# The low parts of the merge weights of the first two branches, taken from GpSimd to VectorE

## The reference

```python
h = x * (1 + scale) + shift
proj = h @ p['w_in'][l]
hy_in, da_q, da_k, da_v, mla_dq, mla_dkv, mla_kr, paths, merge = jnp.split(proj, IN_SPLITS, axis=-1)
...
br = jnp.stack([y_hy, y_da, y_mla], axis=2) * jax.nn.silu(paths.reshape(b, n, N_BRANCH, BR_W))
y_br = jnp.einsum('blni,nid->blnd', br, p['w_branch'][l])
merged = jnp.sum(jax.nn.sigmoid(merge.reshape(b, n, N_BRANCH, D_MODEL)) * y_br, axis=2)
out = merged @ p['w_out'][l]
x = layer_norm(ALPHA * x + gate * out, p['ln_g'][l], p['ln_b'][l])
```

## Time and profile before

| | |
|---|---|
| median of 3 runs | 1846.05 us |
| lowest and highest | 1843.01 and 1846.44 us |
| the profiled execution | 1844.08 us, of which its span is 1842.3 us |
| mean granted TensorE clock | 0.992 |
| PE busy | 1761.0 us, 96% of the span |
| DVE busy | 1142.0 us, 62% |
| ACT busy | 691.7 us, 38% |
| POOL busy | 481.6 us, 26% |

### The profile page before, as it was taken

One profiled execution on the slowest core, in us unless ns is written; L12 is line 12 of the kernel. 1 busy time (PEld: TensorE's weight loads), 2 busy tenths in 40 slices (PEclk: granted clock), 3 DMA queues, 4 the chain that ended last, 5 costly groups with the idle time before them and its releaser, 6 DMA issues.

```text
span 1842.3 us, 28575 instructions
## 1 busy us (share of the span) xinstructions
PE 1761.0 (96%) x11624; PEld 1579.8 (86%) x11624; DVE 1142.0 (62%) x1626; ACT 691.7 (38%) x1186; POOL 481.6 (26%) x234
## 2 busy tenths in 40 slices
PE   5899999999999999999889999999999999999997
PEld 2888799878898888999876969998888898889997
DVE  5599895455354444587878989925544544435755
ACT  3434312444244455322263332224432454542123
POOL 0100033221242212467301000422222411215563
PEclk9999999999999999999999999999999999999999
DMA  9111122111211111353621112212122111114431
GB/s 361 47 58 35 35 92 75 53 52 56 69 35 54 38 54 58 121 200 120 250 92 35 48 45 68 81 49 62 47 67 65 46 53 39 42 58 160 160 109 69
DMA packets 50594, 150.07 MB, mean 81 GB/s; under 512 B 9690, under 2 KB 13914, under 8 KB 49696
## 3 DMA queue, kind: packets, MB, share of 16 engines
q1 hardware_dynamic: 46864, 134.09, 22.2%
q10 hardware_dynamic: 3600, 14.16, 2.2%
HBM read 141.63 MB, written 6.59 MB: 80 GB/s over the span
## 4 chain that ended last, share of the span: by engine, by line
PE 70%; DVE 19%; issue 5%; ACT 2%; POOL 2%; DMA 1%; ACTq 0%; SPq 0%; DVEq 0%; POOLq 0%
PE PS L888 8%; PE PS L889 8%; PE PS L893 8%; PE PS L908 7%; PE PS L914 6%; PE PS L909 6%; PE PS L997 5%; PE PS L986 4%; PE PS L1010 4%; PE PS L1188 2%; PE PS L1028 2%; PE PS L1031 2%; DVE Wl L1689 2%; POOL Wl L2138 1%; DVE work L1662 1%
## 5 line engine op out<-in xcount | busy, mean ns | idle before, releaser
L2138 POOL TENSOR_TENSOR Wl<-W,Wh 128x1024 fp32r<-128x1024 f32 (+3 forms) x176 | 367.5, 2090 | 1201.7 <-ACT Wh L1312 1201.7
L888 PE MATMUL PS<-Hh,Wh 128*128 128x320 f32 x1472 | 439.5, 313 | 16.4 <-ACT Wh L1312 10.1
L889 PE MATMUL PS<-Hl,Wh 128*128 128x320 f32 x1472 | 435.4, 310 | 0.0
L888 PEld LDWEIGHTS PS<-Hh,Wh 128*128 128x128 f32 x1472 | 278.2, 189 | 32.4 <-issue 18.7
L1668 DVE TENSOR_REDUCE st<-PS 128x1 f32<-128x640 f32 (+1 forms) x160 | 114.9, 718 | 287.1 <-PE PS L1010 184.1
L889 PEld LDWEIGHTS PS<-Hl,Wh 128*128 128x128 f32 x1472 | 278.3, 189 | 0.0
L1312 ACT ACTIVATE work<-PS 128x640 f32<-128x640 f32 (+8 forms) x276 | 170.6, 626 | 262.9 <-PE PS L893 87.4
L893 PE MATMUL PS<-Hh,Wl 128*128 128x320 f32 x1472 | 231.0, 309 | 0.7 <-POOL Wl L2138 0.7
L893 PEld LDWEIGHTS PS<-Hh,Wl 128*128 128x128 f32 x1472 | 219.6, 188 | 1.1 <-POOL Wl L2138 0.9
L1312 ACT ACTIVATE Wh<-W 128x1024 fp32r<-128x1024 f32 (+3 forms) x208 | 186.3, 899 | 78.5 <-PE PS L893 26.7
L908 PE MATMUL PS<-Hh,Wh 128*128 128x320 f32 x544 | 168.8, 324 | 1.9 <-ACT Wh L1312 0.8
(11 more groups left out here) (276 smaller groups left out, 3138.9 us busy)
## 6 DMA issues: line engine op xcount, KB each, us to landing
W<-in_w_in SPq DMA_DIRECT2D x132, 512.0 KB, 3.5
W<-in_w_branch SPq DMA_DIRECT2D x48, 256.0 KB, 2.7
work<-in_w_mod_rows ACTq DMA_DIRECT2D x23, 512.0 KB, 3.8
pmod_w<-in_w_mod SPq DMA_DIRECT2D x8, 1024.0 KB, 11.2
W<-in_w_out SPq DMA_DIRECT2D x16, 512.0 KB, 4.4
work<-in_x_sample SPq DMA_DIRECT2D x2, 2048.0 KB
late_modulation_w<-in_w_mod_rows SPq DMA_DIRECT2D x5, 512.0 KB, 6.6
x_mid<-work SPq DMA_DIRECT2D x1, 2560.0 KB, 8.5
```

Of the source, the lines that this page charges most:

```text
L888: pe.matmul(out, Wh[:, b, kk, :], xh[:, kk, t], start=kk == 0, stop=False)
L889: pe.matmul(out, Wh[:, b, kk, :], xl[:, kk, t], start=False, stop=False)
L2138: return pool.tensor_tensor(out, in_, high.bitcast(f32), ALU.subtract)
```

## The change

`low_by_vector` now also gives VectorE the tiles of `mgate` and `mbranch` with index below `2 * KD` = 16, that is of branches 0 and 1. VectorE makes such a low part at the step `mg0` or `mb0` of its tile, where TensorE begins the Wh products; and it makes only the part of the tile that holds weights (`depth`: 8 blocks of 128 for a gate, 4 for a branch).

```diff
 def low_by_vector(l, n):
-    return n in LOWS or n in (0, 1)
+    return n in LOWS or n in (0, 1) or (SPLIT[n][0] in ("mgate", "mbranch") and SPLIT[n][1] < 2 * KD)
...
                 if l or n > 1:
                     dve.wait_ge(*tile_done(l, n - 2))
-                TT(Wl[:, n % 2], W[:, g % NW], Wh[:, n % 2].bitcast(f32), ALU.subtract).then_inc(sems["w_lo"], 1)
+                k = depth(SPLIT[n][0])
+                TT(Wl[:, n % 2, 0:k], W[:, g % NW, 0:k], Wh[:, n % 2, 0:k].bitcast(f32), ALU.subtract).then_inc(sems["w_lo"], 1)
...
                     if (kind, i) in LOW_BETWEEN:
                         low_part(l, LOW_BETWEEN[kind, i])
+                    if kind in ("mg0", "mb0"):
+                        low_part(l, SPLIT_AT["mgate" if kind == "mg0" else "mbranch", i])
                     if kind == "pmod":
```

## The result

The changed kernel takes **1854.82 us** (median of 4 runs, 1853.64 to 1856.2) beside 1845.23 us of the kernel before (4 runs, 1843.01 to 1846.44). The ratio is **1.0051**, with a 95% interval of 1.0038 to 1.0064: it is slower by 9.6 us, more than the 0.2% that can be told from no change. The forecast said slower, 1853.5 us, in a range of 1848.5 to 1857.5.

What follows compares the result with a forecast made beforehand. The prediction took TensorE to bound the kernel. Waits of 3.5 us (units 4, 9, 14), 3.4 (unit 19) and 0.6 (latent attention) sum to 7.5 us, giving a median of 1853.5 us, range 1848.5 to 1857.5.

Steps and rivals of the forecast that it cites:

- TensorE bound, nothing to win by this: Attention stretches: TensorE is busy nearly throughout and waits for none of the 64 moved tiles, so almost nothing to win.
- Units 4, 9, 14: Differential attention: TensorE waits 0.59 us for VectorE's low part behind the division, six times, 3.5 us.
- the three units show the same 0.19: Units 4, 9, 14, both layers: 0.19 to 0.20 us between the division's end and TensorE's first Wl load.
- Unit 19: Differential attention: low part comes behind two divisions, so TensorE waits 1.7 us, twice, 3.4 us.
- the collision: Unit 19: VectorE's small product takes 2.04 us beside GpSimd's low part; expected gone, else the wait is 3.6 us.
- The 128x512 low part: VectorE's low part on that shape, priced at 0.69 us from the same kind of operation; lower bound 0.61.
- The latent attention: Unit 14: mqr's GpSimd low part comes behind VectorE's, so TensorE waits 0.3 us, twice, 0.6; elsewhere nothing.
- The sum: Whole kernel: 3.5 + 3.4 + 0.6 = 7.5 us slower, all carried to the end.
- The clock behind unit 19: After each 1.7 us wait the granted clock may fall, costing 1.3 us more each, up to 1856.1 us.
- Hidden: Rival: TensorE's queue or an existing wait takes up the delays, or low parts come in time; 1846 to 1849, chance 0.13.
- Faster: Rival: VectorE operations stretched by GpSimd become short and TensorE gains; 1843 us, chance 0.03.
- Dearer: Rival: unit 19's collision stays, both clocks fall, or VectorE's waiting holds up maxima and exponentials; 1856 to 1861, chance 0.12.

Runs made afterwards that it cites:

- the longer low parts: Changed kernel with the eight late branch low parts over all eight blocks (128x1024) instead of four: 1859.79 us, 1.0083 to the kernel before.
- the eight alone: Against the kernel before, VectorE takes only the four branch tiles of each layer wanted in units 4, 9, 14 and 19: 1852.87 us, ratio 1.0042.
- the low parts ahead of the division: Changed kernel with the eight late branch low parts made ahead of VectorE's division instead of behind it: 1847.03 us, 1.0007 to the kernel before.
- branch 1 alone: Against the kernel before, VectorE takes only branch 1's low parts (mgate and mbranch 8 to 15), in the latent attention: 1845.5 us, ratio 1.0.
- a repair: Kernel before, with GpSimd making mv's low part ahead of its part of path 6; alone 1845.49 us, ratio 0.9999.

## Why the prediction was right, and where it was off

**TensorE bound, nothing to win by this: right.** All 64 moved, but in time, gave 1.0007 [0.9997 to 1.0017], and 56 of them 1.0004 [0.9995 to 1.0013]. GpSimd's 116 us less are worth nothing, since TensorE waited for none of these tiles.

**Units 4, 9, 14: 0.59 each, 3.5 in all.** Measured 0.56, 0.55, 0.91, 0.56, 0.68 and 0.56: 3.82 us. Four are right to 0.04. The step that failed a little is "the three units show the same 0.19": in unit 14 of layer 0 VectorE's reduction starts 0.95 us behind the start of the weight load of its matmul (431.73 to 432.68) instead of 0.59, and the low part comes 0.3 us later with it. Two traces of the changed kernel and that of the longer low parts have it, that of the eight alone does not. What causes it is open.

**Unit 19: 1.7 each.** Measured 1.66 twice, with the small product at 0.16 us, as said. That GpSimd's tile, now behind VectorE's, takes the collision out of the way could be read off the order of the two. Had the collision stayed, the wait would have been 3.6 us.

**The 128x512 low part: 0.69.** Measured 0.692; the estimate came from a row of another operation on that shape.

**The latent attention: 0.6.** Measured 0.27 at each load, 0.3 from trace to trace. Nothing else in it waits: unit 2 and the gate tiles had the slack that the rows gave.

**The sum: 7.5 us.** The traces give 7.8 us for the change itself. The medians give 9.6 and 9.8 us, with an interval of about 7.0 to 11.8 us, which holds both. That the forecast of 1853.5 us lies only 1.3 us below the 1854.82 measured is partly luck: it was added to a median of three runs, 1846.05 us, which the fourth run brought to 1845.23, and this 0.8 us hides a part of the 2.1 us by which the sum is short.

The clocks of the runs say where the 2 us are. In the 57 runs of the kernel before that stand beside the experiments the mean granted clock is 0.9897 on average, and a run with a clock lower by 0.001 takes 1.5 us more (a straight line through them, correlation -0.77). The nine runs of the changed kernel have 0.9882 on average; 0.0015 less clock is 2.2 us by this line (an estimate), and of 9.2 us between the means 7.0 are left. The eight low parts alone run at 0.9896, as the kernel before does, and their mean is 7.0 us above it, where the list of loads has 6.6 us of waits. The longer low parts have 0.9880 beside 0.9894: 2.2 us of their 14.3, and 12.1 are left, where the loads have 11.4 and unit 14 of the latent attention 0.5. So, by this estimate, the waits explain what stays at equal clock, and the sum lacks a term for the clock, which the prediction had in its range (up to 1856.1) and not in its sum. No run tests why the clock is lower there. Two candidates are in the traces. One is the start at a lower clock, 2.4 to 3.4 us in two of two traces of the changed kernel, but also in the traces of two kernels as fast as the one before (the low parts ahead of the division, and branch 1 alone). The other is drops of the clock of about 1.5 us, which fall at differing places from trace to trace. The runs do not settle which.

**The clock behind unit 19: not lost.** The page of stretches has 1.00 behind both waits of 1.66 us; the 1.3 us each that I kept in the range did not come. Behind the waits of 2.19 us it came once in two. The term was of the right size, about 1.3 to 1.5 us for a fall of the clock, but it had the place wrong.

**The rivals.** *Hidden* is refuted: the waits are in the time, and each 0.54 us more on the eight comes out at the end. *Faster* is refuted in a telling way: VectorE's stretched operations do become short (2.04 to 0.16 us, 18 us over the program), and nobody waited for them. *Dearer* would have needed the collision or the clock in unit 19, and neither came.

## What to carry to other kernels

Before an instruction is moved to an engine that works in order, compare two times of the trace for each place where it lands: the end of what stands ahead of it there plus its own length, and the start of what consumes it. Here 56 of 64 places had room and cost nothing that the medians show (two of them made a GpSimd tile behind them 0.3 us late); eight had 0.2 us of room or less, and made nearly all of the loss. The busy share of an engine (62% against 26%) says nothing about that. When a late operand is brought forward, another can become the late one: at `mv` VectorE's `kv_lo` was ready at 549.23 us, and at 551.87 us once GpSimd's low part had moved beside it. So look at which engine the moved instruction will now run beside. And a gain that is read off one stretch of two traces needs the stretches around it: the half clock that left unit 16 stood behind `mv`.

## What was not expected of the hardware

- Four operations of VectorE end only after the GpSimd instruction beside them: 3.13 us instead of 0.89 and 2.22 instead of 0.16 in the kernel with the early low parts, 4.99 instead of 2.94 for two at `mv`. I knew it from unit 19, but not that it would undo a repair. The starts do not order them cleanly: the operation of 3.13 us begins 0.03 us ahead of GpSimd's, and is stretched all the same.
- The length of a wait alone does not tell whether the clock falls. TensorE's waits of 1.66 us in unit 19 left it at 1.00 in all six places of three traces (the changed kernel twice, the eight alone). Those of 2.19 us left it so in one layer and were followed by 0.58 in the other. The 1.54 us in unit 16 were followed by half clock in layer 0 in all ten traces that have them, and in layer 1 in six of ten. Where this wait was taken away, the clock fell behind the one for `mv`, about 2 us, in four of four places.
- So the price of a short wait can't be read off the wait that stands ahead of a fall: taking 2.5 us of idle time away won 6.2 us by the medians, and 2.9 us in the trace over the two waits.
